# Gate/up projections of two feed-forward blocks as 7 block products in place of 8

## The reference

```python
def swiglu_ffn(h, w_gu, w_down):
    g, u = jnp.split(h @ w_gu, 2, axis=-1)
    return (jax.nn.silu(g) * u) @ w_down
...
    for i in range(DEPTH):
        x = x + 0.5 * swiglu_ffn(rmsnorm(x, n_ffn1[i]), ffn1_w_gu[i], ffn1_w_down[i])
...
        x = x + mix
        x = x + mem_cross_attn(rmsnorm(x, n_xattn[i]), rmsnorm(mem, n_mem[i]),
                               x_w_q[i], x_w_kv[i], x_w_o[i])
        x = x + 0.5 * swiglu_ffn(rmsnorm(x, n_ffn2[i]), ffn2_w_gu[i], ffn2_w_down[i])
    return rmsnorm(x, n_final)
```

## Time and profile before

| | |
|---|---|
| median of 3 runs (lowest, highest) | 1993.27 us (1992.75, 1993.96) |
| span of the profiled execution | 1992.3 us; it has no other time of its own |
| TensorE busy | 1983.5 us, 100% |
| TensorE weight loads | 1654.4 us, 83% |
| DVE busy | 930.9 us, 47% |
| ACT busy | 710.2 us, 36% |
| POOL busy | 160.8 us, 8% |
| read from memory | 203.23 MB, 107 GB/s |

### The profile page before, as it was taken

How to read it: one execution, slowest core, us unless ns; L and a number is a source line. 1 busy time by engine, 2 the same in 40 slices (tenths; PEclk the granted TensorE clock), 3 DMA queues, 4 the chain that set the end, 5 groups by cost and what they waited for, 6 DMA issues and landing times.

```text
span 1992.3 us, 23096 instructions
## 1 busy us (share of the span) xinstructions
PE 1983.5 (100%) x9182; PEld 1654.4 (83%) x9182; DVE 930.9 (47%) x1007; ACT 710.2 (36%) x865; POOL 160.8 (8%) x201
## 2 busy tenths in 40 slices
PE   9999999999999999999999999999999999999998
PEld 7888888888898888888888888888898888888887
DVE  5343443487865654434343443433287544434323
ACT  5222232256554543222222322222156443322222
POOL 2000001100112120000001000000112022200000
PEclk9999999999999999999999999999999999999999
DMA  5323352323434533232223323222353324432221
GB/s 176 105 88 102 100 142 76 104 64 106 129 126 127 169 106 106 84 105 88 96 95 100 106 84 105 87 98 95 121 165 114 103 85 127 158 105 96 94 95 74
DMA packets 204153, 214.53 MB, mean 108 GB/s; under 512 B 21970, under 2 KB 186960, under 8 KB 204096
## 3 DMA queue, kind: packets, MB, share of 16 engines
q1 hardware_dynamic: 180416, 192.95, 29.6%
q0 software_dynamic: 6432, 17.64, 3.4%
q10 hardware_dynamic: 17248, 3.16, 0.9%
HBM read 203.23 MB, written 10.49 MB: 107 GB/s over the span
## 4 chain that ended last, share of the span: by engine, by line
PE 96%; DVE 1%; DMA 1%; ACT 1%; issue 1%; SPq 0%; ACTq 0%; POOL 0%; DVEq 0%
PE ps L368 32%; PE ps L369 32%; PE ps L370 32%; DMA p_scratch<-sq 0%; ACT w_hi L1198 0%; DVE w_lo L1731 0%; DMA raw<-in_ffn_w_gu 0%; DVE sums L2213 0%; DMA p_tok<-p_scratch 0%; DVE sums L2233 0%; SPq L390 0%; DVE up L2411 0%; SPq L418 0%; PE ps L943 0%; PE ps L1138 0%
## 5 line engine op out<-in xcount | busy, mean ns | idle before, releaser
L368 PE MATMUL ps<-h_hi,w_hi 128*128 128x512 f32 (+1 forms) x1728 | 667.3, 386 | 0.2 <-DVE h_lo L1734 0.2
L369 PE MATMUL ps<-h_lo,w_hi 128*128 128x512 f32 (+1 forms) x1728 | 665.8, 385 | 0.0
L370 PE MATMUL ps<-h_hi,w_lo 128*128 128x512 f32 (+1 forms) x1728 | 665.8, 385 | 0.0
L1731 DVE TENSOR_TENSOR w_lo<-raw,w_hi 128x2048 fp32r<-128x2048 f32 (+4 forms) x195 | 417.4, 2141 | 461.8 <-ACT w_hi L1198 461.8
L1198 ACT ACTIVATE w_hi<-raw 128x2048 fp32r<-128x2048 f32 (+4 forms) x195 | 347.6, 1783 | 271.0 <-PE ps L370 266.9
L368 PEld LDWEIGHTS ps<-h_hi,w_hi 128*128 128x128 f32 x1728 | 324.7, 188 | 65.8 <-DVE h_lo L1734 0.9
L370 PEld LDWEIGHTS ps<-h_hi,w_lo 128*128 128x128 f32 x1728 | 324.6, 188 | 64.8
L369 PEld LDWEIGHTS ps<-h_lo,w_hi 128*128 128x128 f32 x1728 | 324.7, 188 | 64.0
L368 PE MATMUL ps<-mid_hi,w_hi 128*128 128x512 f32 x528 | 205.6, 389 | 0.0
L370 PE MATMUL ps<-mid_hi,w_lo 128*128 128x512 f32 x528 | 205.5, 389 | 0.0
L369 PE MATMUL ps<-mid_lo,w_hi 128*128 128x512 f32 x528 | 205.5, 389 | 0.0
(11 more groups left out here) (361 smaller groups left out, 1909.2 us busy)
## 6 DMA issues: line engine op xcount, KB each, us to landing
raw<-in_ffn_w_gu SPq DMA_DIRECT2D x87, 1024.0 KB, 5.1
raw<-in_ffn_w_down SPq DMA_DIRECT2D x34, 1024.0 KB, 4.9
raw<-in_x_w_kv SPq DMA_DIRECT2D x16, 1024.0 KB, 5.9
raw<-in_gla_w_in SPq DMA_DIRECT2D x12, 1024.0 KB, 5.1
raw<-in_ffn_w_down SPq DMA_DIRECT2D x12, 768.0 KB, 4.3
raw<-in_x_w_q SPq DMA_DIRECT2D x8, 1024.0 KB, 4.9
raw<-in_x_w_o SPq DMA_DIRECT2D x8, 1024.0 KB, 6.1
raw<-in_gla_w_out SPq DMA_DIRECT2D x8, 512.0 KB, 3.5
```

The lines of the kernel that those rows point to most:

```text
L368: nc.tensor.matmul(out_ap, left[0], right[0], start=first, stop=False)
L369: nc.tensor.matmul(out_ap, left[0], right[1], start=False, stop=False)
L370: return nc.tensor.matmul(out_ap, left[1], right[0], start=False, stop=last)
L1731: return nc.vector.tensor_tensor(out_ap, value, hi.bitcast(F32), ALU.subtract)
```

## The change

For n = 1 and 2, each gate/up slot but the first holds one gate block and one up block (128 + 128 columns, by two DMAs of 128-column pieces). Seen as a 2x2 matrix of blocks (rows 0 to 3 and 4 to 7; gate and up) times a 2x2 matrix of h (the same halves of rows; tokens 0 to 255 and 256 to 511), the slot is computed by 7 products of sums of blocks, as in the method of Strassen and Winograd. Such a slot is called **mixed** here. Each product takes 4 rows x 3 = 12 matmuls of 256 columns; products and their weight operands (**forms**) are numbered 0 to 6 as in the code.

- Forms: forms 1, 2, 4 and 6 are sums of weight blocks (`w_sums`, 4 sums of 512 elements per partition), made on DVE for all slots but the first of a run, where POOL makes them. Each of the 7 forms is split on its own, by an ACT and a DVE instruction of 512 elements. The 7 forms fill the space of both halves of w_hi and w_lo but one eighth, so form i of a slot is made when product i of the slot before is done. `leading` is the number of forms (3 for n = 1, 4 for n = 2) that fit beside the plain slot ahead of a run.
- Sums of h: four for each of 4 row pairs (`sum_x`, `x_sums_lo`, with `scale_x` and `x_sums_hi` on ACT: a scaled copy of 512 elements and a hi part of 1024), made in `feed_last_pairs` during the last two pairs of the block before. Product 1 of the first mixed slot waits for them.
- Results: ACT copies product 0 to bank b (`SEEDED`, product 2 waits for it) and product 1 to `sq` (`P5_TAKEN`); DVE adds them to bank d (`U4_SEEDED`, product 4 waits), scales the low gate half (`C11_TAKEN`), adds into `sq` (`C22_READY`, product 6 waits), multiplies (`C12_TAKEN`), scales the high gate half (`C21_TAKEN`) and multiplies it (`gated_high`, step GATED); ACT and DVE split the result into `half_hi`, `half_lo`.
- The block is run in two parts of 11 slots: gate/up of a part (`mixed_run`: 10 mixed slots, 11 in the second part), then `down` of that part as 4 pairs of 6 + 5 rows. The scaled results are added to x twice, after each part.
- Unchanged: n = 0 and 3, mixers, cross attention. Plain slots now take the half of w_hi and w_lo that `area` says.

```diff
+    def place_mixed(n):
+        for part in range(2):
+            for s in range(part * HALF, (part + 1) * HALF):
+                if s == 0:
+                    place(("gu", n, 0), 2, 2, C, loads=2)
+                else:
+                    if s in (1, HALF):
+                        mixed_first[n, part] = len(mixed_slots)
+                    place(("gu", n, s), 0, 0, C, mixed=True, loads=2)
+            for pair in range(C // 2):
+                for g, (_, rows) in enumerate(HALF_GROUPS):
+                    place(("down", n, part, pair, g), 2, 2 if g == 1 else 0, rows)
...
+        def form(parts, w, i):
+            spot = (i, (i + 4) % PRODUCTS)[area[w]]
+            flat = parts[:].rearrange("p s k n -> p (s k n)")[:, spot * KH * P:(spot + 1) * KH * P]
+            return flat.rearrange("p (k n) -> p k n", n=P)
...
+                                  .then_inc(raw_loaded[w % 2], 16)
+                        for pair in range(C // 2):
+                            for g, (row, nrows) in enumerate(HALF_GROUPS):
+                                load_fixed(("down", n, part, pair, g), down[layer], part * HALF + row, nrows, pair * COLS)
...
+            def mixed_slot(n, part, l, j=None):
+
...
+                for i, bank in enumerate((6, 7, b, 6, b, d, b)):
+                    if i < 6:
+                        pe.wait_ge(sig.form_lo_ready, count(6, OPENED + 6 * m + i + 1))
+                    else:
+                        pe.wait_ge(sig.w_lo_ready, count(1, w + 1))
+                    if i == 0 and m > 0:
+                        pe.wait_ge(sig.mixed_dve_step, count(6, dve_step(m - 1, C11_TAKEN)))
+                    if i == 1:
+                        if m > 0:
+                            pe.wait_ge(sig.mixed_act_step, count(3, act_step(m - 1, P5_TAKEN)))
+                        if (part, l) == (0, 0):
+                            pe.wait_ge(sig.x_sums_ready, OPENED + KH * (MIXED.index(n) + 1))
+                    if i == 2:
+                        pe.wait_ge(sig.mixed_act_step, count(3, act_step(m, SEEDED)))
+                    if i == 4:
+                        pe.wait_ge(sig.mixed_dve_step, count(6, dve_step(m, U4_SEEDED)))
+                    if i == 6:
+                        pe.wait_ge(sig.mixed_dve_step, count(6, dve_step(m, C22_READY)))
+                    hi, lo = form(w_hi, w, i), form(w_lo, w, i)
+                    for kk in range(KH):
+                        right_hi, right_lo = activation_form(i, kk)
+                        to, fresh = ps[:, bank, 0:TH], i < 2 and kk == 0
+                        nc.tensor.matmul(to, hi[:, kk, :], right_hi, start=fresh, stop=False, skip_group_check=True)
+                        nc.tensor.matmul(to, hi[:, kk, :], right_lo, start=False, stop=False, skip_group_check=True)
+                        last = nc.tensor.matmul(to, lo[:, kk, :], right_hi, start=False, stop=kk == KH - 1,
+                                                skip_group_check=True)
+                    last.then_inc(sig.product_done, 1)
+
...
+            def mixed_run(n, part):
+
...
+                def low_mid_hi(s):
+                    act.wait_ge(sig.mixed_dve_step, dve_step(m0 + s - max(part * HALF, 1), GATED))
+                    hi_part(half_hi[:, s % HALF, :], t[:, s % 2, :]).then_inc(sig.mid_hi_ready, 1)
+
+                for m in range(m0, end):
+                    l, s = m - m0, m - m0 + max(part * HALF, 1)
...
+                        act.wait_ge(sig.evacuated, (o - 2 + 2 * l) if part == 0 else o - 1)
+                    if l >= 2:
+                        act.wait_ge(sig.mixed_dve_step, dve_step(m - 2, C21_TAKEN))
+                    nc.scalar.activation(ps[:, (even, odd)[l % 2], 0:TH], ps[:, 6, 0:TH], ACT.Copy)\
+                      .then_inc(sig.mixed_act_step, 1)
+                    if l == 0:
...
+                        low_mid_hi(s - 1)
+                    act.wait_ge(sig.product_done, OPENED + PRODUCTS * m + 2)
+                    if l >= 2:
+                        act.wait_ge(sig.mixed_dve_step, dve_step(m - 2, C22_READY))
+                    hi_part(sq[:, s % 2, TH:], ps[:, 7, 0:TH]).then_inc(sig.mixed_act_step, 1)
+                    following = m + 1 if m + 1 < end else None
+                    w = mixed_slots[m] + 1
+                    if following is not None:
+                        for i in range(4):
...
+                                 slot_rows[w], sig.product_done)
+                    act.wait_ge(sig.mixed_dve_step, dve_step(m, C11_TAKEN))
+                    nc.scalar.activation(t[:, s % 2, 0:TH], t[:, s % 2, 0:TH], ACT.Silu).then_inc(sig.mixed_act_step, 1)
+                    if following is not None:
+                        for i in range(4, PRODUCTS):
+                            form_hi(following, i, sig.product_done, OPENED + PRODUCTS * m + i + 1)
+                    act.wait_ge(sig.mixed_dve_step, dve_step(m, C21_TAKEN))
+                    nc.scalar.activation(t[:, s % 2, TH:], t[:, s % 2, TH:], ACT.Silu).then_inc(sig.silu_done, 1)
+                split_hi((w + 1) % 2, area[w + 1], loaded[w + 1], OPENED + PRODUCTS * end, slot_rows[w + 1],
+                         sig.product_done)
+                low_mid_hi(s)
+
...
+            def sum_x(f, kk):
+
+                step = 4 * (KH * (3, 4).index(f) + kk)
+                low, high = slice(0, TH), slice(TH, SEQ)
+                dve.wait_ge(sig.x_scaled_ready, OPENED + step // 4 + 1)
+                if step > 0:
+                    dve.wait_ge(sig.x_sums_ready, OPENED + step // 4)
+                nc.vector.scalar_tensor_tensor(x_sums[:, 0, :], x[:, kk + KH, high], gain(f, kk + KH), x_scaled[:, high],
+                                               ALU.mult, ALU.add).then_inc(sig.x_sum_step, 1)
+                nc.vector.tensor_tensor(x_sums[:, 2, :], x_scaled[:, low], x_scaled[:, high], ALU.subtract)\
+                  .then_inc(sig.x_sum_step, 1)
+                dve.wait_ge(sig.x_sum_step, OPENED + step + 1)
+                nc.vector.tensor_tensor(x_sums[:, 1, :], x_sums[:, 0, :], x_scaled[:, low], ALU.subtract)\
+                  .then_inc(sig.x_sum_step, 1)
+                dve.wait_ge(sig.x_sum_step, OPENED + step + 3)
+                nc.vector.scalar_tensor_tensor(x_sums[:, 3, :], x[:, kk + KH, low], gain(f, kk + KH), x_sums[:, 1, :],
+                                               ALU.mult, ALU.subtract).then_inc(sig.x_sum_step, 1)
...
+            def feed_last_pairs(f, pair, split_after, residual):
+
...
+                else:
+                    m = mixed_slots.index(split_after + 2)
+                    residual(6)
+                    feed(f, 6)
+                    x_sums_lo(f, 1)
+                    residual(7)
+                    feed(f, 7)
+                    sum_x(f, 2)
+                    form_lo(m, 0)
+                    x_sums_lo(f, 2)
+                    sum_x(f, 3)
+                    form_lo(m, 1)
+                    x_sums_lo(f, 3)
+                    for i in range(2, leading(split_after + 2)):
+                        form_lo(m, i)
...
+            def mixed_run(n, part):
+
...
+                def gated_high(m, s):
+                    dve.wait_ge(sig.silu_done, FC * n + s + 1)
+                    dve.wait_ge(sig.mixed_dve_step, dve_step(m, C22_READY))
+                    nc.vector.tensor_tensor(t[:, s % 2, TH:], t[:, s % 2, TH:], sq[:, s % 2, 0:TH], ALU.mult)\
+                      .then_inc(sig.mixed_dve_step, 1)
...
+                    else:
+                        gated_high(m - 1, s - 1)
+                        half_mid_lo(s - 1)
+                    if following is not None:
+                        weight_sums(following, (0, 1))
+                        form_lo(following, 0)
+                    dve.wait_ge(sig.product_done, OPENED + PRODUCTS * m + 3)
+                    dve.wait_ge(sig.mixed_act_step, act_step(m, P5_TAKEN))
+                    nc.vector.tensor_tensor(ps[:, d, 0:TH], ps[:, b, 0:TH], sq[:, s % 2, TH:], ALU.add)\
+                      .then_inc(sig.mixed_dve_step, 1)
+                    if following is not None:
+                        weight_sums(following, (2, 3))
+                        form_lo(following, 1)
+                    dve.wait_ge(sig.product_done, OPENED + PRODUCTS * m + 4)
+                    if s >= 2:
+                        dve.wait_ge(sig.mid_ready, FC * n + s - 1)
+                    if (part, l) == (1, 0):
+                        dve.wait_ge(sig.x_half_ready, OPENED + C * (MIXED.index(n) + 1))
+                    nc.vector.tensor_tensor(t[:, s % 2, 0:TH], ps[:, 6, 0:TH], rms[:, 0:TH], ALU.mult)\
+                      .then_inc(sig.mixed_dve_step, 1)
+                    if following is not None:
+                        form_lo(following, 2)
+                    dve.wait_ge(sig.product_done, OPENED + PRODUCTS * m + 5)
+                    if m >= 2:
+                        dve.wait_ge(sig.mixed_dve_step, dve_step(m - 2, GATED))
```

(24 more changed lines are left out.)

379 lines of the change are left out of this document (351 added, 28 removed).

## The result

The changed kernel takes 2015.85 us (median of 4 runs, 2015.32 to 2016.08) against 1993.05 us before in the same comparison: ratio 1.0113, 95% interval 1.0099 to 1.0127, so it is slower by 1.1%. Its profiled run has a span of 2013.9 us, 21.6 more than 1992.3. The predicted 2013 lies 3 us off. That it is so near is in part luck: two terms of the sum were off by 8 to 9 us each, with opposite signs.

What follows compares the result with a forecast made beforehand. TensorE was taken as the bound (96% of the chain), its slot gain eaten by a DVE loop; 1992.3 - 3.4 - 3.2 + 0.9 + 22.4 + 2.7 = 2011.7, median 1.0 over: 2013 us. Range 2000 to 2040.

Steps and rivals of the forecast that it cites:

- TensorE's own time: Mixed slot: 84 matmuls of 256 columns at 0.12 us, 10.08 us against 10.88; 33.6 us at most over 42 slots.
- The steady slot, 10.78: Mixed runs: a loop over DVE through product 6 makes a slot 10.78 us, not 10.08; 34 slots give -3.4 us.
- the walk: DVE's work followed in order from the end of product 6 of one slot to the next, and through the starts.
- The last and first slots of the runs: Last slots have no forms or wait, 4 x -0.80 = -3.2; first slots of second parts cost +0.8 and +0.1.
- The starts, +22.4: Starts of n = 1 and 2: TensorE waits for DVE at the norm and first mixed slot; 22.4 us for both.
- POOL's sums lie ahead of the forms that need them: First mixed slots: POOL's weight sums were listed as hidden work, with no term in the sum.
- The end of block 3, +2.7: End of n = 2, in down: the next group's w_lo comes at 17.7 after 14.96 us of matmuls; TensorE waits 2.7.
- The rival with a colder start: Both first mixed slots: the clock falls, products 4 to 6 take twice as long, +8.6 us, 2022; chance 0.1.
- The rival without overlap on DVE: Steady slots: DVE loses its 0.09 overlap each time, 1.6 us a slot, +51, 2064 us; chance 0.12.
- The rival with cheaper starts: Block starts: half of 22.4 is lost elsewhere anyway or the order of waits is too strict, 2002 us; chance 0.12.

Runs made afterwards that it cites:

- e1: Changed kernel with half_lo on DVE made after weight sums 0 and 1 of the next slot; 2000.89 us, ratio 1.0039 to the kernel before.
- e4: Changed kernel with the band's split on ACT and DVE moved behind a weight group's split at the third block's end; 2013.00 us, ratio 1.0097 to the kernel before.
- e5: Changed kernel with 36 thrown-away matmuls of 512 columns on TensorE ahead of each of two norms; 2015.24 us, ratio 1.0111 to the kernel before.
- e2: Changed kernel with the four weight sums of each block's first mixed slot on DVE, not POOL; 2011.01 us, ratio 1.0089 to the kernel before.
- e7: Changed kernel with edits of e1, e2, e4, earlier acc_parts split, earlier norm root and reciprocal, inv_count moved; 1986.79 us, ratio 0.9966 to the kernel before.

## Why the prediction was right, and where it was not

The median lies 1.9 us over the span of the profiled run and not 1.0 (2015.74 and 2013.9), which is 0.9 of the 3 us; the rest, 2013.9 against 2011.7, is what the terms leave when their errors are added up.

- **TensorE's own time** (0.12 us for 256 columns, 10.08 a slot): right, shown by e1 to the hundredth.
- **The steady slot, 10.78:** the mechanism was right (a loop over DVE through product 6, with half_hi inside), the size was not: 10.54. The term that was mis-sized is the handovers. I took 0.13 and 0.17 us between DVE and ACT and 0.29 from TensorE; here gated_high ends at 814.19 and half_hi starts at 814.23, it ends at 814.86 and half_lo starts at 814.89: 0.04 and 0.03. TensorE's last product reaches DVE 0.20 behind its end. That is 0.23 + 0.09 = 0.32 less; from C22_READY (820.92) to the end of product 6 it took 1.64 and not 1.60, and the rest is rounding. 34 x (10.54 - 10.88) is -11.6 and not -3.4. The right handovers stood in the prediction's own rows: in the earlier trace rows DVE's x ends at 1092.46 and ACT starts at 1092.49, ACT ends at 1093.21 and DVE starts at 1093.25. With these 0.03 and 0.04 the walk gives 10.55. Why it was longer in the earlier trace rows no run here shows; the order of the old loop has an ISA row ahead of each mid_lo, which the new code has not, and that was not tested.
- **The last and first slots of the runs**, -3.2 and +0.9: right. Without down (+0.4) the runs gave -13.7: 34 x -0.34 = -11.6, and -2.1 for these, where -2.3 was forecast.
- **The starts, +22.4:** right in mechanism, measured +31.2. The step that failed is that POOL's sums were put at nothing ("POOL's sums lie ahead of the forms that need them"). I asked when they are done, not whom they hold up. Counted off the rows of DVE, the instructions beside POOL's work (four additions and an s_lo in each block) are 4.9 us longer than their prices in the second block and 4.1 in the third. The second smaller part is inv_count, 1.2 us of DVE ahead of acc_parts in the second block, which the walk left out. The third is the clock: 0.4 us from norm to scaled result in each block. That is 6.5 and 4.5, against 5.1 and 3.6 that the starts were off, so other prices of the walk were 1.4 and 0.9 too high in sum; the handovers between DVE and ACT, 0.23 in each of its two rounds, are a part, and the rest was not followed.
- **The end of block 3, +2.7:** TensorE's wait is 2.3, near the forecast. The 6.5 us between memory's end and w_hi in the earlier trace rows, which I took over without naming them, are mostly ACT's wait for POOL's band, which e4 shows as the cause here. The 1.6 us of lower clock behind the wait had no term. Together +4.1.
- **The rival with a colder start:** its condition held. The clock fell at both starts (the granted clock is 0.50 from 753 to 757), as the earlier trace rows could not show. The Trainium skill, page "TensorE: Matmul & The Clock Gate", section "Why this matters for your kernels", says that idle gaps put the clock back, and the trace agrees for these stands of 10.8 and 9.3 us. Its price did not hold: it assumed that TensorE sets the end of these slots (e5).
- **The rival without overlap on DVE:** out; 512 elements start 0.60 apart here too, though each lasts 0.68, and the slot is 10.54 and not over 11.5.
- **The rival with cheaper starts:** out; they cost 31.2 and not half of 22.4.

The stall of DVE beside POOL is told by the rows above: a DVE addition of two operands in SBUF ends 0.28 us behind POOL's. The Trainium skill, page "SBUF — State Buffer", section "Who interferes with whom", states it as a rule: a DVE instruction with two SBUF inputs contends with a GpSimd instruction that reads SBUF, and the one that comes second is blocked until the first has ended. The trace agrees that they hold each other up, POOL's sums too (1.65 us for the fourth, where the first took 1.31). On who waits it agrees but for one pair: DVE's row of 738.26 starts ahead of POOL's of 738.93 and was held all the same; starts on POOL are rough. So the engines do not wait for each other only through semaphores, as the first section has it.

The trace of the kernel before had shown this, in the pool mixer, 5 us behind the earlier trace rows:

```profile
1507.86 9.55 POOL L557 TENSOR_TENSOR acc<-acc,sq 128x512 f32<-128x512 f32 x5 [2.72 <-ACT sq L1226]
...
1510.15 2.97 DVE L1731 TENSOR_TENSOR w_lo<-raw,w_hi 128x2048 fp32r<-128x2048 f32 x1 [0.34 <-ACT w_hi L1198]
1513.04 1.77 DVE L1734 SCALAR_TENSOR_TENSOR h_lo<-x,cols,h_hi 128x512 fp32r<-128x512 f32 x1
```

Beside five additions on POOL (1.91 us each, where one alone takes 1.34) w_lo takes 2.97 us and not the 2.29 of the earlier trace rows, and h_lo 1.77 and not the 0.75 of the earlier trace rows. The price of work on POOL could have been read there.

What stays open: e5 left 2.7 us unfilled in the second block, so what the clock costs there was not measured by itself; why a handover between DVE and ACT takes 0.03 us in one place and 0.13 in another; and that DVE's first addition of each third round (1.05 at 737.28) is long because of POOL's addition of squares rests on the ends (0.27 us behind POOL's here, 0.29 in the third block and in e2), since no run moved that addition. e7 makes six edits at once, so its two new ones have no price of their own.

## What to carry to other kernels

When a faster product moves work to an engine with time to spare, walk that engine's queue once round the loop: a loop with an empty handover in it is cured by putting independent work there (one line, 15 us here). Price the starts apart from the loop: a gain of 0.34 us in each of 34 slots was lost in two starts. What makes a start long is the queue's order and too little work on the bound engine to cover it; one more slow slot there was worth more than the fast one that it replaced.
